# Moving the one-hot comparisons of a sparse expert pass from VectorE to GpSimd

## What is computed

```python
s = jnp.einsum('thpd,hpkd->thpk', q, sub_keys)      # two scores of 128 keys a head
sv, si = lax.top_k(s, K)                            # K = 16
cand = sv[:, :, 0, :, None] + sv[:, :, 1, None, :]
cv, ci = lax.top_k(cand.reshape(t, PEER_HEADS, K * K), K)
idx = i1 * PEER_KEYS + i2                           # 16 experts a head, 8 heads a token
g = jax.nn.softmax(cv, axis=-1)
u = expert_down[idx]
act = jax.nn.gelu(jnp.einsum('thkd,td->thk', u, xb))
```

## Time and profile before

| what | before |
|---|---|
| median of 3 runs | 4108.4 us (4105.47 to 4109.06) |
| profiled execution | 4111.73 us, its span 4110.0 us |
| PE busy | 3846.8 us (94%) |
| DVE busy | 2647.5 us (64%) |
| ACT busy | 1692.5 us (41%) |
| POOL busy | 1784.0 us (43%) |
| granted TensorE clock, mean | 0.972 |

### The profile page before, as it was taken

How to read it: one execution, slowest core, us unless ns; L and a number is a source line. 1 busy time by engine, 2 the same in 40 slices (tenths; PEclk the granted TensorE clock), 3 DMA queues, 4 the chain that set the end, 5 groups by cost and what they waited for, 6 DMA issues and landing times. The chain is left out here.

```text
span 4110.0 us, 58100 instructions
## 1 busy us (share of the span) xinstructions
PE 3846.8 (94%) x21214; PEld 3214.6 (78%) x21214; DVE 2647.5 (64%) x4884; ACT 1692.5 (41%) x3247; POOL 1784.0 (43%) x1275
## 2 busy tenths in 40 slices
PE   8899999989899969978999999999969999999998
PEld 3688888856677769978999999999956777677776
DVE  3455411138775425689999989997756666666666
ACT  2123343358422431125777777777611222222222
POOL 0233333349544212123333233335447677676774
PEclk9999999999999989989999999999979999999999
DMA  8222233357566332167888888899999999999998
GB/s 308 53 78 97 97 102 100 103 180 253 180 183 200 103 128 61 49 226 242 255 265 273 262 276 272 268 286 351 359 308 339 347 352 347 334 341 350 343 345 295
DMA packets 639573, 956.46 MB, mean 233 GB/s; under 512 B 198996, under 2 KB 416740, under 8 KB 638436
## 3 DMA queue, kind: packets, MB, share of 16 engines
q1 hardware_dynamic: 319492, 423.09, 31.3%
q0 software_dynamic: 110592, 402.70, 28.1%
q10 hardware_dynamic: 209248, 127.55, 10.0%
HBM read 807.33 MB, written 145.88 MB: 232 GB/s over the span
## 5 line engine op out<-in xcount | busy, mean ns | idle before, releaser
L1909 POOL DMA_INDIRECT down_rows<-in_peer_down_dram,row_ids x384 | 451.3, 1175 | 856.7 <-DVE row_u L2049 769.7
L1930 PE MATMUL p_u<-h2T_hi,downT_hi 128*128 128x320 f32 x2048 | 656.8, 321 | 11.7 <-ACT gelu_out L1980 11.7
L1930 PE MATMUL p_u<-h2T_lo,downT_hi 128*128 128x320 f32 x2048 | 636.9, 311 | 0.0
L1930 PE MATMUL p_u<-h2T_hi,downT_lo 128*128 128x320 f32 x2048 | 636.0, 311 | 0.0
L2049 DVE CUSTOM_DVE_ANT_0 gate_rows<-down_rows,x_tok_rows 128x1024 f32<-128x1024 f32 x384 | 469.1, 1222 | 84.9 <-DMA down_rows<-in_peer_down_dram,row_ids 72.0
L2451 PE MATMUL p_y<-up_hi,coef_hi 128*128 128x512 f32 x1240 | 494.2, 399 | 19.3 <-DVE coef_lo L2343 9.2
L2451 PE MATMUL p_y<-up_lo,coef_hi 128*128 128x512 f32 x1240 | 486.5, 392 | 0.0
L2451 PE MATMUL p_y<-up_hi,coef_lo 128*128 128x512 f32 x1240 | 484.7, 391 | 0.0
L517 PE MATMUL p<-hT_hi,w_hi 128*128 128x512 f32 x1024 | 405.6, 396 | 0.0
L1930 PEld LDWEIGHTS p_u<-h2T_hi,downT_hi 128*128 128x128 f32 x2048 | 388.8, 190 | 13.9 <-issue 13.8
L517 PE MATMUL p<-hT_hi,w_lo 128*128 128x512 f32 x1024 | 399.3, 390 | 0.0
(11 more groups left out here) (355 smaller groups left out, 8105.1 us busy)
## 6 DMA issues: line engine op xcount, KB each, us to landing
down_raw<-in_peer_down_dram SPq DMA_DIRECT2D x128, 512.0 KB, 5.9
up_raw<-in_peer_up_dram SPq DMA_DIRECT2D x128, 512.0 KB, 5.8
scratch_gu<-gelu_out ACTq DMA_DIRECT2D x128, 320.0 KB, 5.4
gelu_in<-scratch_gu SPq DMA_DIRECT2D x128, 320.0 KB, 5.3
weights_in<-scratch_w SPq DMA_DIRECT2D x128, 320.0 KB, 6.9
w_raw<-in_w_in_dram SPq DMA_DIRECT2D x64, 512.0 KB, 3.9
w_ada_sb<-in_w_ada_dram SPq DMA_DIRECT2D x12, 2048.0 KB, 14.5
scratch_w<-weights_out ACTq DMA_DIRECT2D x40, 512.0 KB
```

Source lines behind the costliest of these rows:

```text
L1909: pool.indirect_dma_start(out=rows[:, c % RING, :], out_offset=None, in_=inp["peer_down"][0], in_offset=bass.IndirectOffsetOnAxis(ap=row_i ...
L1930: mm = pe.matmul(ps_u[half][:, 0:HD], d[:, n % 3, k, :], h2[h][:, k, half * HD:(half + 1) * HD], start=(j == 0), stop=(j == 3 * KD - 1))
```

## The change

`second(g)` is taken out of VectorE's list and put into GpSimd's. VectorE keeps `keep_picks`. On GpSimd the granule's one comparison of 128 x 512 becomes four comparisons of 128 x 128, one a token, each against a scalar per partition. GpSimd's list was the plain sequence of the 384 fetches; now it is ordered by tiles: the first four fetches, then for each tile the fetches that follow its dots, and then the comparisons for the next tile's granules. The waits of `second` go with it. Its semaphore still counts one a granule.

```diff
 @block.gpsimd
 def _(pool):
-    for c in range(TA):
+    def fetch(c):
         ...
+    def second(g):
+        w = g // IN_BLOCK
+        if g % IN_BLOCK == 0:
+            pool.wait_ge(picks_ready, 4 * w + 4)
+        if g >= 2:
+            pool.wait_ge(w_mm, g - 1)
+        for t in range(QB):
+            c = g * QB + t - w * P
+            hit = pool.tensor_scalar(b_[:, g % 2, t, :], iota[:], picks[:, w % 2, 2, c:c + 1], None, ALU.is_equal)
+        hit.then_inc(second_ready, 1)
+    for c in range(RING):
+        fetch(c)
+    for n in range(E1):
+        for c in dots_of(n):
+            if c + RING < TA:
+                fetch(c + RING)
+        for g in granules_of(n + 1):
+            second(g)
 @block.vector
-    def second(g):
-        w = g // IN_BLOCK
-        if g % IN_BLOCK == 0:
-            keep_picks(w)
-            dve.wait_ge(picks_ready, 4 * w + 4)
-        if g >= 2:
-            dve.wait_ge(w_mm, g - 1)
-        at = slice(g * QB - w * P, (g + 1) * QB - w * P)
-        dve.tensor_tensor(b_[:, g % 2], picks[:, w % 2, 2, at].unsqueeze(2).to_broadcast([P, QB, P]),
-                          iota[:].unsqueeze(1).to_broadcast([P, QB, P]), ALU.is_equal).then_inc(second_ready, 1)
     for n in range(E1):
         ...
         for g in granules_of(n + 1):
-            second(g)
+            if g % IN_BLOCK == 0:
+                keep_picks(g // IN_BLOCK)
```

## The result

The changed kernel takes 4198.56 us (median of 4 runs, 4196.6 to 4200.47) where the kernel before takes 4107.0: a ratio of 1.0223 with an interval of 1.0205 to 1.024. It is 2.2% slower. Predicted were 4080 us, 28 less, in a range of 4052 to 4128.

A forecast was written before the change was run, and what follows sets the result against it. VectorE's list, with the comparison at its end, was taken to pace PE in the first stretch. 40 + 4 - 5 - 8 - 3 = 28 us less gave 4080 us, in a range of 4052 to 4128.

The forecast's parts named there:

- The holding: First stretch: GpSimd's packs of comparisons hold VectorE's two-operand operations, 0.6 us a tile; charged 8 us.
- The price: A GpSimd comparison of 128 x 128 takes 0.33 us, within bounds of 0.28 to 0.68 us.
- 40 of the 45 us: First stretch: of 45 us lost to PE's waits for the comparison, 40 go because it ends earlier.
- The late stretch: Down pass after the selection ends, paced by the ring: comparisons end later on GpSimd, fetches may queue behind; charged 3 us.
- far from full: GpSimd has room: 211 us of comparisons beside 451 us of fetches in a pass of 1250 us.
- VectorE's list sets the pace: First stretch: VectorE needs 9.8 us a tile against PE's 9.2; its last operation, the comparison, delays PE.
- The 30.1 us before the weights: First stretch: PE's waits put down to "issue" are really for `second_ready`, the operation that moves.
- A: Rival: holding and price win, VectorE still sets the pace; slower, 4157 us at 0.50 us a comparison; chance 0.24.
- B: Rival: ScalarE takes VectorE's place, waits become gelu or first-factor waits; no difference, 4104 to 4112 us; chance 0.12.
- C: Rival: VectorE runs ahead, all is cured and the clock returns to 1.00; 60 us less, 4048; chance 0.08.
- The dots' maximum: Sign: the maximum of VectorE's dots rises above 1.2 us, their mean by less than 0.2.
- p_w <- issue: Sign: PE's waits of this kind before the weights fall from 30 us to under 8.

The follow-up runs named there:

- both comparisons: Kernel before, plus 640 GpSimd comparisons into a spare buffer that nobody waits for; VectorE still makes the real ones: 4178.78 us, ratio 1.0189.
- VectorE late: Changed kernel, but from granule 126 on VectorE makes the comparisons in their old place: 4159.79 us, ratio 1.0136.
- The last experiment: Kernel before, with VectorE's comparisons and `keep_picks` placed ahead of the selection instead of behind it: 4066.79 us, ratio 0.9905.

## Why the prediction was wrong

**The failed steps** are two, the larger one first. The prediction has a term for VectorE held by GpSimd's packs and none for GpSimd's comparisons held by VectorE's dots; and it takes 0.33 us for a comparison.

**The holding** was seen, and charged to one side only: 8 us, for VectorE's operations held by GpSimd's packs. The runs show both sides. VectorE's operations were held by 29 us in the first stretch, 0.34 us a tile where 0.6 were reckoned, and never to the end of a pack: no dot was lengthened by more than 0.28 us. GpSimd's comparisons were held by 143 us, and the sum has nothing for it. With a VectorE operation of one operand in the dot's place the ratio is 0.9992 instead of 1.0223, so this term is worth some 95 us. One row of the up pass, in which a VectorE operation waited for two of GpSimd's, was read as the general case.

By the Trainium skill (SBUF — State Buffer, section Who interferes with whom) the one that issues second waits for the whole of the first, whichever engine that is. The trace agrees for comparisons that start while a dot runs: they end 0.46 to 0.48 us behind it. It does not agree for the other order: of 134 dots that started while a comparison ran, 94 kept their length and 40 gained 0.28 us at most. So for this comparison the measurement decides: the loss falls on GpSimd's operations of 0.6 us, which stand beside dots of 1.2 us, and little of it on the dots.

**The price** stands in the second paragraph on GpSimd's work: "I take 0.33, near the rows of the same size". It measured 0.603 without holding. The bounds, 0.28 to 0.68, held it; the choice went by the nearest rows in size (a cast, a select). The 640 x 0.33 = 211 us are 520 us with the holding. With 0.603 the prediction's own sum reads: comparisons end 1.5 + 2.4 = 3.9 us after the last dot with one granule and 1.5 + 4.8 = 6.3 with two, against 3.7 and 6.1 before. So the price alone used up the earlier place, worth "40 of the 45 us" in the sum, and what holding adds makes them later than they ever had been: the pack shown above took 6.5 us, not 4.8. But the price alone doesn't make the kernel slower, as the run with a reduction in the dot's place shows. And the right price would not have saved the forecast: comparisons cheaper by 159 ns gained 36 us, which on a straight line is 61 us at 0.33 us a comparison (an estimate), and leaves the kernel some 30 us slower than before.

**The late stretch** was charged 3 us and cost 47. The step said that "the fetch after the next dot may stand behind it. PE shifts once against the ring". It never summed GpSimd's list. Per tile of the late stretch this has 4 fetches, their gaps and 136 / 23 = 5.9 comparisons: 240 / 23 = 10.4 us of work where a tile took 218 / 23 = 9.5. At the 0.33 us of the forecast the same list would have had (98 + 19) / 23 + 5.9 x 0.33 = 7.0, and at the measured 0.603 without holding 8.7, which still fits. So it is the holding, with a mean of 918 ns here, that fills the list; the run without it takes 229.9 us. GpSimd was called "far from full" by a mean over the pass (211 + 451 of 1250 us), which was the wrong stretch to ask. The kernels with both comparisons (+44) and with VectorE late (0) show that it is GpSimd's load.

**What VectorE's list is worth.** "VectorE's list sets the pace, and the comparison at its end passes that on to PE": the second half held, the first did not. The last experiment leaves VectorE 807 us busy and takes 840. The 30.1 us before the weights were indeed `second_ready`, as the 0.11 us behind the comparison said. The 45 us put down to it were somewhat high: 30 us return without comparisons at all, and 42 by the place, with `keep_picks` moved as well.

**The rivals.** A gave slower, 4157 us at 0.50 us a comparison, with a chance of 0.24. The sign came as it said, the mechanism only in part. The selection was held, the dots were not, and VectorE didn't set the pace: it waits 135.7 us for ScalarE, three times as much as before. At 0.444 us a comparison, where A has about 4130, the kernel took 4163. A has 5 us for the late stretch, where 47 were lost, and this is the size of the 41 us by which even its number is short. B, ScalarE takes the place of every wait, didn't come: where the comparisons are out of the way the gelu waits do rise, from 9.6 to 17.4 and 21.2 us, but 30 and 42 us are gained. C, all cured, 4048: its nearest is the comparison ahead of the selection, 4066.8, on VectorE.

**The signs named ahead.** Of "it would be wrong if a comparison takes over 0.4 us, if the dots' mean rises by 0.3 us or more, or if the weights wait for GpSimd in most tiles", the first came true, the second did not, the third in 44 waits over 87 tiles, about half. The dots' maximum rose, to 1.50 us, and their mean by 0.02, as expected. "p_w <- issue", to fall under 8 us, rose to 69.9.

**Left open.** Why this form takes twice as long as a cast of the same size; why a comparison that has begun seldom holds a dot; how the gain of the last kernel divides. One comparison of four tokens on GpSimd instead of four was not tried.

## What to carry over

Before work is moved to an engine, sum that engine's list per tile in the fullest stretch, at the upper bound of the unknown price, with the fetches that it issues and with what its operations may be held for: a mean over the pass hides a full list. When a timeline shows that an operation is late, first try to issue it earlier on the engine that has it: here this gave 0.95% where moving it lost 2.2%. Where a row shows one engine held by another, ask also what the reverse would cost: here the engine with many short operations was held by the one with long ones, by 99 us in the first stretch, and the other way round it was 29.

## What the runs showed of the hardware

A `tensor_scalar` of 128 x 128 on GpSimd takes 603 ns with its scalar in memory, 535 with a constant, 598 as an addition and 444 with 64 columns, where a cast and a select of 128 columns take 289 and 284.

A GpSimd comparison that starts while a VectorE dot of two operands runs (1.22 us) ends 0.46 to 0.48 us after it; the longest took 1.835 us, and 2.289 where VectorE also compared. Beside a reduction of one operand and the same length 593 of 640 keep their 0.60 us.

The other way round, a dot that starts while a comparison runs is lengthened by 0.28 us at most, and in 94 of 134 cases not at all. VectorE's short operations pay more: 128 x 16 columns with one operand went from 168 to 328 ns in the median, and up to 654.

After two waits of 1.9 us within a tile the granted clock was 0.74 for 4 us. Over 87 tiles, with 32 us more of waits, it was 0.96 instead of 0.98, and TensorE was busy 20 us longer for the same work.
